# The first projection block of a two-model kernel, with its modulation made in quarters

## The reference, cut to what matters

```
shift, scale, gate = split(silu(c) @ ada_w[0] + ada_b[0], 3)         # x
cshift, cscale, cgate = split(silu(c_ctx) @ ada_w[0] + ada_b[0], 3)  # ctx
hx = rmsnorm(x, norm_g[0]) * (1 + scale) + shift
hc = rmsnorm(ctx, norm_g[0]) * (1 + cscale) + cshift
u, g = split(h @ pool_w_in[0], 2)          # 1024 -> 2048 columns
y = (group_matmul(centred_means(u) - u) * pool_scale * silu(g)) @ pool_w_out
x = x + gate * y
```

## Time and profile before

| | us |
|---|---|
| median of 3 runs (1820.13 to 1821.28) | 1820.42 |
| the profiled execution | 1821.5 |
| its span, first to last instruction | 1819.7 |
| TensorE busy | 1799.0 (99%) |
| GpSimd busy | 1365.3 (75%) |
| VectorE busy | 941.8 (52%) |
| ScalarE busy | 905.6 (50%) |

### The profile page before, as it was taken

One profiled execution on the slowest core, in us unless ns is written; L12 is line 12 of the kernel. 1 busy time (PEld: TensorE's weight loads), 2 busy tenths in 40 slices (PEclk: granted clock), 3 DMA queues, 4 the chain that ended last, 5 costly groups with the idle time before them and its releaser, 6 DMA issues.

```text
span 1819.7 us, 25066 instructions
## 1 busy us (share of the span) xinstructions
PE 1799.0 (99%) x9322; PEld 1483.2 (82%) x9322; DVE 941.8 (52%) x1755; ACT 905.6 (50%) x1337; POOL 1365.3 (75%) x568
## 2 busy tenths in 40 slices
PE   6999999999999999999999999999999999999999
PEld 5888788877889888887888888888888878888887
DVE  4673766778754524866553230713095865143152
ACT  3324424764455644456554644564445565545452
POOL 2624544559968898977689798969897858888885
PEclk9999999999999999999999999999999999999999
DMA  9853885748776675565466566567655645656663
GB/s 367 295 202 93 277 301 162 197 144 308 243 273 201 211 221 192 178 198 167 134 189 187 182 195 191 194 187 234 193 191 184 190 137 164 192 160 212 189 196 127
DMA packets 200553, 366.61 MB, mean 201 GB/s; under 512 B 32852, under 2 KB 54084, under 8 KB 199876
## 3 DMA queue, kind: packets, MB, share of 16 engines
q1 hardware_dynamic: 197568, 357.52, 62.8%
q10 hardware_dynamic: 2884, 7.73, 1.1%
HBM read 364.12 MB, written 6.13 MB: 203 GB/s over the span
## 4 chain that ended last, share of the span: by engine, by line
PE 98%; DVE 1%; DMA 0%; ACT 0%; ACTq 0%; POOL 0%; issue 0%
PE ps L1247 26%; PE ps L1249 26%; PE ps L1248 26%; PE ps L1373 3%; PE ps L1374 3%; PE ps L1375 3%; PE ps L1938 1%; PE ps L1939 1%; PE ps L1940 1%; PE ps L1295 1%; PE ps L1865 1%; PE ps L1644 1%; PE ps L1615 1%; PE ps L1505 1%; PE ps L1625 1%; PE ps L1910 1%
## 5 line engine op out<-in xcount | busy, mean ns | idle before, releaser
L613 POOL TENSOR_TENSOR w_lo<-raw,w_hi 128x1024 fp32r<-128x1024 f32 x556 | 1346.4, 2457 | 404.4 <-ACT w_hi L651 383.0
L1247 PE MATMUL ps<-w_hi,act_rows_r 128*128 128x512 f32 x2064 | 816.1, 395 | 4.0 <-POOL w_lo L613 3.3
L1249 PE MATMUL ps<-w_hi,act_rows_r 128*128 128x512 f32 x2064 | 805.9, 390 | 0.0
L1248 PE MATMUL ps<-w_lo,act_rows_r 128*128 128x512 f32 x2064 | 805.4, 390 | 0.0
L651 ACT ACTIVATE w_hi<-raw 128x1024 fp32r<-128x1024 f32 x556 | 572.0, 1058 | 370.1 <-DMA raw<-in_ffn_w_up 99.6
L1247 PEld LDWEIGHTS ps<-w_hi,act_rows_r 128*128 128x128 f32 x2064 | 388.4, 188 | 92.0 <-issue 8.8
L1249 PEld LDWEIGHTS ps<-w_hi,act_rows_r 128*128 128x128 f32 x2064 | 388.2, 188 | 81.8
L1248 PEld LDWEIGHTS ps<-w_lo,act_rows_r 128*128 128x128 f32 x2064 | 388.6, 188 | 77.2
L2593 DVE STREAM_TRANSPOSE ps<-proj 32x256 f32<-32x256 f32 (+1 forms) x384 | 166.6, 434 | 6.5
L2574 DVE TENSOR_TENSOR proj<-proj,ps 128x1024 f32<-128x1024 f32 (+1 forms) x18 | 20.4, 1132 | 252.2 <-PE ps L1249 247.8
L1373 PE MATMUL ps<-act_rows_r,w_hi 128*128 128x512 f32 (+1 forms) x288 | 101.4, 352 | 0.0
(11 more groups left out here) (244 smaller groups left out, 1557.1 us busy)
## 6 DMA issues: line engine op xcount, KB each, us to landing
raw<-in_w_in SPq DMA_DIRECT2D x120, 512.0 KB, 3.8
raw<-in_ffn_w_gate SPq DMA_DIRECT2D x88, 512.0 KB, 4.4
raw<-in_ffn_w_up SPq DMA_DIRECT2D x88, 512.0 KB, 4.4
raw<-in_ffn_w_down SPq DMA_DIRECT2D x88, 512.0 KB, 4.2
proj<-in_ada_w SPq DMA_DIRECT2D x39, 512.0 KB, 8.0
pt<-in_ada_w SPq DMA_DIRECT2D x38, 512.0 KB, 6.4
raw<-in_pool_w_in SPq DMA_DIRECT2D x32, 512.0 KB, 8.0
raw<-in_na_w_in SPq DMA_DIRECT2D x32, 512.0 KB, 5.0
```

The lines of the kernel that those rows point to most:

```text
L613: pool.tensor_tensor(w_lo[:, s, :], raw[:, s, :], w_hi[:, s, :].bitcast(F32), ALU.subtract).then_inc(lo_done, 1)
L1247: pe.matmul(o, h, hi, start=start, stop=False)
L1248: pe.matmul(o, h, lo, start=False, stop=False)
L1249: return pe.matmul(o, c, hi, start=False, stop=stop)
```

## The change

- The first four modulation blocks are cut anew. Block a now holds 256 columns of the shift and 256 of the scale, a quarter of each, so `ADA_ORDER` goes, and each piece of 512 KB is sent as two loads with rows of 1 KB.
- `first_gains(q)` works on one block: VectorE transposes it in PSUM, multiplies the two scale columns by norm_g in PSUM, adds the bias to the shift columns into `mods`, and adds (1 + bias) * norm_g, made once ahead, to the scale columns into `gains`.
- All four tiles are turned in four units of two pieces. `turn_bank` and the modulation products rotate through banks 2, 3, 6 and 7 (`FIRST_BANKS`); the products of quarter q and the unit of tile 3 share a bank.
- The order is written by quarters: all four tiles go through a quarter's columns, then through the next, with the last two tiles of a quarter behind the modulation products of the next. Before, x went through half of the columns, then ctx, then both through the other half.
- Loads: c and c_ctx come first, with a transpose of their own, then ada_b and norm_g, then x tile 0. The six other parameter tensors are issued by ScalarE behind the condition columns. x tile 1 and the two ctx tiles are issued by the sync engine. Parameters land in `bias` and no longer in `proj`, so the sync engine no longer waits for them. Both of ScalarE's tables (Silu, Sqrt) are loaded ahead with a dummy operation.
- GpSimd no longer waits for the first gains. The squares' discarded output goes elsewhere in `proj`.

```diff
-ADA_ORDER = (0, 2, 1, 3) + tuple(range(4, DEPTH * ADA_COLS))
+FIRST_BANKS = (2, 3, 6, 7)
 def turn_bank(key, t, u):
     if key == "p0":
-        return ((4, 5, 6, 7), (6, 7, 2, 3), (6, 6), (7, 7))[t][u]
+        return FIRST_BANKS[(5 * u + 1 + t) % 4]
 # sync engine
+                    if a < ADA_FIRST:
+                        for part in range(2):
+                            n0 = part * D + 256 * a
+                            sp.dma_start(free(ada_slot(k, a), [[512, 2], [1, 256]], 256 * part), v[:, 2 * k:2 * k + 2, n0:n0 + 256])
+                        continue
...
+                        if stage == "p0_in" and g == 0:
+                            ada_weights(0, (3,))
+                            rows(1, x_res[:, 1, :], "x")
+                            for t in range(NT, 2 * NT):
+                                rows(t, free(proj[:, 0:1], [[1, D]], CTX_RES + (t - NT) * D), "ctx")
+                            ada_weights(1)
                         if stage == "p0_in" and g == 1:
-                            sp.dma_start(free(proj[:, 0:1], [[D, NT], [1, D]], CTX_RES),
                             ada_weights(2)
+                        if stage == "p0_in" and g == 2:
                             ada_weights(3)
-            ada_weights(0)
-            ada_weights(1, (0, 1))
-            sp.wait_ge(param_in, 16 * PARAMS)
-            ada_weights(1, (2, 3))
+            ada_weights(0, range(3))
 # GpSimd
-            pool.wait_ge(dve_done, dve_s.count(("first_gains", 0, 1)))
 # ScalarE
+            act.wait_ge(x_in[0], 16)
+            rms("p0", 0, stream(0))
+            split(1)
+            high_of_tile("p0", 0, some=(0,))
+            for t in range(1, 2 * NT):
+                act.wait_ge(x_in[t], 16)
                 rms("p0", t, stream(t))
+            for t in range(1, 2 * NT):
+                high_of_tile("p0", t, some=(0,))
+            split(1)
+            for u in range(1, 4):
+                for t in range(2 * NT):
+                    high_of_tile("p0", t, some=(u,))
                 split(1)
+            split(1)
 # TensorE, start()
+                products(0)
+                turn_unit(0, 0)
                 part(0, 0)
+                pe.wait_ge(param_in, 16 * PARAMS)
+                pe.wait_ge(dve_done, dve_s.count("mod_cols"))
+                pe.transpose(ps[:, 5, 0:112], bias[0:112, 0:P], ident[0:112, 0:112])
+                turn_unit(1, 0)
+                turn_unit(2, 0)
                 part(1, 0)
+                pe.wait_ge(ada_read, 1)
+                turn_unit(3, 0)
+                for u in range(1, 4):
+                    turn_unit(0, u)
+                    products(u)
+                    part(2, u - 1)
+                    turn_unit(1, u)
+                    part(3, u - 1)
+                    turn_unit(2, u)
+                    part(0, u)
+                    pe.wait_ge(ada_read, u + 1)
+                    turn_unit(3, u)
+                    part(1, u)
+                part(2, 3)
+                part(3, 3)
 # VectorE
+            def first_gains(q):
+                bank = FIRST_BANKS[5 * q % 4]
+                dve.wait_ge(ada_used, 4 * q + 4)
+                dve.transpose(ps[:, bank, P:2 * P], ps[:, bank, 0:P])
+                g = free(ps[:, bank, 0:1], [[32, 2], [1, 2]], P + 64)
+                dve.tensor_tensor(g, g, free(cols[:, 0:1], [[1, 2], [0, 2]], C_NORMG + 2 * q), ALU.mult)
+                dve.tensor_tensor(mods[:, 2 * q:2 * q + 2, 0:2], free(ps[:, bank, 0:1], [[32, 2], [1, 2]], P),
+                                  free(cols[:, 0:1], [[1, 2], [0, 2]], C_ADAB + 2 * q), ALU.add)
+                dve.tensor_tensor(free(gains[:, 0:1, 0:1, 0:1], [[KC, 2], [1, 2]], 2 * q),
+                                  free(ps[:, bank, 0:1], [[1, 2], [32, 2]], P + 64),
+                                  free(cols[:, 0:1], [[0, 2], [1, 2]], C_ADAB + 8 + 2 * q), ALU.add)
```

More of the change, by code:

```diff
@@ L222, in program @@
         acc_free = [sem("acc_free0"), sem("acc_free1")]
[L223 removed]
+        mod_in = sem("mod_in")
+        cond_in, param_in, const_in = sem("cond_in"), sem("param_in"), sem("const_in")
+        x_in = [sem(f"x_in{t}") for t in range(2 * NT)]
         bias_in = [sem("bias_in0"), sem("bias_in1")]
@@ new lines, in products @@
+                def products(u):
+                    bank = FIRST_BANKS[5 * u % 4]
+                    read_out(bank)
+                    ada_products(u, bank)
+                products(0)
+                turn_unit(0, 0)
+                part(0, 0)
+                pe.wait_ge(param_in, 16 * PARAMS)
+                pe.wait_ge(dve_done, dve_s.count("mod_cols"))
+                pe.transpose(ps[:, 5, 0:112], bias[0:112, 0:P], ident[0:112, 0:112]).then_inc(pe_done, pe_s.one("cols"))
+                held[5] = (dve_s, "cols")
@@ L1447, in blocks @@
+                part(2, 3)
+                part(3, 3)
+                for bank in tuple(held):
+                    read_out(bank)
             def blocks(stage, n, nw, key, tiles=(0, 1)):
```

192 lines of the change are left out of this document (84 added, 108 removed).

## The result

The changed kernel takes 1822.43 us (median of 22 executions, 1821.40 to 1829.25), the kernel before 1820.46 (22 executions beside it, 1819.76 to 1824.33); the ratio is 1.0012, 95% interval 1.0007 to 1.0018. That is 0.12% slower, inside the 0.2% that I called no change, but above the range that I gave (1816.2 to 1821.3). Its profiled execution took 1821.73 us, with a span of 1819.9.

A forecast was written before the change was run, and what follows sets the result against it. TensorE, busy 99%, was taken as the bound, with gains possible only in the first 24 us. First group 7.45 earlier, less give-backs, put the second column block at 54.05 instead of 55.43: 1.4 gained, 1819.0 us, range 1816.2 to 1821.3.

The forecast's parts named there:

- First group: 16.1: First block: the first projection group starts at 16.1 us instead of 23.55, a gain of 7.45.
- I take 0.25, since the second row is from a stretch of thin traffic: 12.25: First modulation block's loads: 1 KB rows cost 0.25 us, bounded by 0 and 1.0, so products start at 12.25.
- That is 3.3 us from the end of the first group, 2.7 of them TensorE's hole.: First quarter: the second group comes late, at 22.2 us, queued on VectorE behind the parameter copy.
- (4) The clock: Second group: the hole keeps TensorE's clock low, costing 1.0 us, bounds 0 and 2.7, bringing the sum to 53.7.
- nothing gained: Rival, first block: clock stays low through the second modulation block, 1.7 us more, 0.4 hidden; 1820.3 us, chance 0.13.
- warm start: Rival, first block: clock already high when the first group begins and stays; 2.9 us less, 1816.1 us, chance 0.15.
- So a new wait of 0.35 for the low half: Start of second column block: the fifth weight group's split comes late, so TensorE waits 0.35 us, starting at 54.05.
- What I cost at nothing: Later quarters: VectorE's 2.9 us chain is covered by 3.3 us of TensorE work; later modulation and weights arrive in time.
- the slower rival: Later quarters: VectorE's chain outlasts its cover, holes of 1 us in each of three; 6.6 us more, 1825.6, chance 0.05.
- 1821.5 - 1.4 = 1820.1 in its terms, 1819.0 in terms of the median: Whole kernel: 1.4 us gain taken from the profiled execution, which was 1.1 above the median 1820.42.
- I carry a shift of that point one to one to the end.: Behind 55.43 us: same work and order, no TensorE wait of a microsecond, so the second block's shift reaches the end.
- late data: Rival, first block: x tile 0 or first weights land after 13 us; at 2.0 us late 1821.0, chance 0.07.

The follow-up runs named there:

- wide_rows: Changed kernel with the first four modulation blocks loaded as before, in 2 KB rows, one load a piece (output not the reference's): 1820.09 us, ratio 0.9990 to the kernel before.
- in_turn: Changed kernel with one added wait near 590 us, holding a GpSimd product until VectorE's first x_res product with the final gains is made: 1823.02 us, ratio 1.0010.
- again_after: Changed kernel run and traced once more, no edit: 1822.96 us, ratio 1.0010 to the kernel before.
- after_filled: Changed kernel with 26 idle identity transposes on TensorE in the waits of the first block: 1823.71 us, ratio 1.0011 to the kernel before.
- fifth_early: Changed kernel with the split of the fifth weight group moved between the second and third tile of the last quarter: 1821.01 us, ratio 1.0002.
- after_look1: Changed kernel, one more profiled execution, no edit: 1822.27 us.
- pair: Changed kernel with tiles 0 and 1 side by side through the first quarter and the parameter transpose and copy moved later: 1819.03 us, ratio 0.9989.
- pair_fifth: pair with the fifth high half of the following weights made earlier by ScalarE, among the last quarter's: 1818.06 us, ratio 0.9985 to the kernel before.
- filled_look1: pair_fifth with 19 idle transposes on TensorE in the first quarter's two long waits, one further execution: 1829.08 us.
- filled_look2: Same kernel as filled_look1, one more execution: 1829.01 us.

## Why the prediction was wrong, step by step

- "First group: 16.1". It was 17.48 (17.3 to 18.1 in five traces). The sum behind the products is right: 3.74 us from the last products to the group, put at 3.85. ScalarE's leg was hidden, as I said: w_lo was ready at 15.59, and what its split waited for at 12.11 was the landing of the weights. But the data's term failed: "I take 0.25, since the second row is from a stretch of thin traffic: 12.25". The products began at 13.74, and wide_rows shows 1.38 of this for the rows of 1 KB and their sends, past even my upper bound of 1.0. I had priced the rows and put the four more sends at nothing. By the Trainium skill (DMA: Bandwidth & Descriptors, Specifications) rows from 512 B on go at line rate, and the term would be 0; the trace disagrees, with 355 GB/s for 390, and decides.
- "That is 3.3 us from the end of the first group, 2.7 of them TensorE's hole." Measured 23.30, 1.1 after my 22.2, and so the same lateness less 0.3. The holes are 0.88 and 1.07 with one turn of two transposes between them.
- "(4) The clock ... I take 1.0". In the profiled execution the sum seems to hold: 54.05, the first group's lateness of 1.38 and 0.23 of longer wait are 55.66, and it was 55.67. That is luck. in_turn, with no low clock behind 23.28, has its block at 54.12, so the fall from 24.10 to 27.50 cost 1.55 and not 1.0. The work from the second group to the wait took 30.1 us at the higher clock (23.28 to 53.38 in in_turn), 0.4 less than my 30.5, and the second group was 1.1 late, not 1.38; the errors nearly cancel. In again_after the clock rose only at 28.75 and the block began 0.86 later still. My rival "nothing gained" describes such executions, and its condition, little work ahead of the second group, was the one that held. after_filled is the rival "warm start" brought about by hand: its block is 2.9 before that of the change's first trace, just that rival's price, but without the total that went with it.
- "So a new wait of 0.35 for the low half": 0.58 idle (0.74 from start to start), at the place named, for the reason named (fifth_early removes it).
- "What I cost at nothing": no wait of TensorE in the later quarters is over 0.2 us; the slower rival's mechanism never appeared.
- "1821.5 - 1.4 = 1820.1 in its terms, 1819.0 in terms of the median". This step failed by 1.1. The profiled execution of before was 1.1 above its median because of the clock in the very block that I rewrote; its usual second column block is at 54.4. My 54.05 was thus 0.4 ahead of before and not 1.4, and with my own numbers the forecast was 54.05 + 1764.2 + 1.8 = 1820.1.
- "I carry a shift of that point one to one to the end." In 14 of 20 traces the rest is 1764.1 to 1764.7, and so it held in most of them; in wide_rows it is 1.4 more, in again_after 5.4, and with idle work in the changed block 3.8 to 11.4 more in four of five traces. I had looked for waits of a microsecond behind the block, found none, and took this for slack. It was an order in which VectorE and GpSimd just did not hinder TensorE.

So two steps failed: the base that I subtracted from, and the term for the loads of the first modulation block. From 1819.0 to the 1821.7 of the profiled execution there are 1.1 for the base and 1.6 for the block, the latter 1.4 of late data and 0.2 of longer wait, with the cancelling errors of (4) inside. The median lies 0.7 above that execution. In after_look1, the trace nearest to it, the excess is in the block (56.21), with later data and another place of the low clock; how much of it is due to the places behind the block in other executions, the runs do not separate. What I hadn't formed is that two of my rivals, late data and low clock, come together.

## What to carry to other kernels

A single profiled execution that lies above the median has its excess somewhere: find the place before subtracting it, since the change may rewrite it. Price more sends apart from shorter rows: here nearly all of the late data was late before the queue was full, while the sends, 0.5 us each, were going out. When a start is brought forward, order the work so that the engine has two pieces in a row at the first opportunity and nothing that can wait stands between: pair, which does both, won 0.11% and pair_fifth 0.15% over the kernel before with the very work with which the change lost 0.12%. And when a forecast meets the trace to 0.01 us, redo its terms one by one before you believe them.

## What the runs showed of the hardware

- A VectorE product with two SBUF inputs, 0.69 us by itself, took 7.33 to 7.35 us beside GpSimd's back-to-back products in four traces (again_after, after_filled, filled_look1, filled_look2), and 2.67 to 2.70 at the same place in the other sixteen.
- TensorE's clock can fall behind a hole, within dense work: in filled_look1 the wait of 2.44 us ended at 360.83, and the granted clock was 0.50 from 361.41 to 364.80; in the change itself the hole ended at 23.30, and the fall was at 24.10. It can also fall within the hole: in the two traces of the kernel before, whose wait of 3.1 us ended at 23.55 and 23.57, it fell at 21.97 and 23.21.
- The same first block had its clock low behind the second group's start for none, 3.4 or 5.6 us in three traces (in_turn, the change, again_after), which put its end at 54.12, 55.67 and 56.53.
- The granted clock in the windows reads 1.00 ahead of the first rise although the matmuls there begin 0.43 us apart (again_after, 17.32 to 26.86), so the column by itself hides the first low stretch.
- ScalarE issued six loads (5.70 to 8.75 us) while its table load and a first activation ran (5.90 to 7.40), so my 2.7 us for them were not on its path: 

```profile
5.70 0.33 ACTq L667 DMA_DIRECT2D bias<-in_ffn_norm  x1
5.90 1.28 ACT L680 ACT_TABLE_LOAD   x1
...
8.36 0.39 ACTq L667 DMA_DIRECT2D bias<-in_conv_db  x1
9.53 1.06 ACT L691 ACTIVATE proj<-x_res 128x1024 f32<-128x1024 f32 x1 [2.13 <-DMA x_res<-in_x]
```
